# A decoder trunk in float32 on one core: the forget gates of its linear attention turned to features on partitions

## The chip, the core and the metric

One core of one Trainium2 chip runs the whole program in one launch. The metric is device time in microseconds, the median over several runs. Engines are named as the profile names them: PE is TensorE (matmuls; PEld its weight loads), ACT is ScalarE, DVE is VectorE, POOL is GpSimd, and SP issues the DMAs.

## The reference

Two layers over 16 meta tokens and 256 tokens of width 1024. Layer 0 is FFN, short convolution, FFN; layer 1 is FFN, gated linear attention (GLA), FFN; after each stands a residual with a layer norm. The change is in GLA alone, which has 4 heads with 128 key features each and chunks of 64 tokens:

```python
q, k, v, g, gz = jnp.split(h @ w_in, splits, axis=-1)
log_a = jax.nn.log_sigmoid((gz @ w_gate_up + b_gate).astype(f32)) / GLA_GATE_NORMALIZER   # / 16
...
b = jnp.cumsum(to_chunks(log_a, GLA_HEAD_K), axis=3)          # restarts in each chunk
b_ref = b[:, :, :, GLA_CHUNK // 2:GLA_CHUNK // 2 + 1, :]
b_last = b[:, :, :, -1:, :]
scores = jnp.einsum('nbhik,nbhjk->nbhij', q * jnp.exp(b - b_ref), k * jnp.exp(b_ref - b))
...
q_inter = q * jnp.exp(b)
k_state = k * jnp.exp(b_last - b)
decay = jnp.exp(b_last[:, :, :, 0, :])
# per chunk: o = q_inter @ state; state = decay * state + k_state^T v
```

The 272 tokens are one short chunk (the 16 meta tokens) and four chunks of 64.

## The kernel before

All activations lie transposed, features on partitions and tokens on the free axis. Every matrix product is done in three rounds with the operands split into a high and a low part (`hi`, `lo`), so a tile of 128 output features by 272 tokens takes 8 x 3 = 24 matmuls. The weights come as units of 128 x 1024: SP loads a unit into one of 4 raw buffers, ACT rounds it to `weights_hi` (L431, `split_hi`), DVE subtracts to get `weights_lo` (L753, `split_lo`), PE uses it (L1214 to L1216). Both split copies form a ring of 8 units, so unit j + 8 is split while the unit of tile j is used or gone. SP loads unit n as soon as `split_lo` of unit n - 4 is done. Every engine has its own instruction list in program order, with semaphores between them. Nothing reorders it: an instruction that waits holds all that stands behind it on its engine.

The GLA stage has 25 tiles, j = 0 to 24: j = 0 is the low-rank gate input gz, 1 to 4 the keys (`kT`), 5 to 8 the queries (`qT`, 256 tokens only), 9 to 16 the values, 17 to 24 the output gate. Tiles 0 to 3 are multiplied before the layer norm's statistics are known (L1239 to L1241, banks 0 to 3) and "unfolded" afterwards by DVE (L829 to L834); ACT then writes them out (L633), which counts in `gla_evac`, as the evacuation of each later tile does (L640, L642, L647). Tile 4 goes to PSUM bank 7, the tiles from 5 on to banks 0 and 1 in turn. So PE may begin tile j only when ACT has evacuated tile j - 2, by the wait for `gla_evac` ahead of each tile.

Between the tiles stand the steps of the gate. After tile 4 PE makes the gate logits with tokens on partitions (L1380: three matmuls of 512 columns, for 16, 128 and 128 tokens), DVE copies them out and takes -|x| (L1089, L1091), ACT does Exp (L662, at j = 5) and Ln(1 + x) (L666, at j = 6), DVE forms the log sigmoid (L1098, at j = 6), and PE sums it within chunks by a matmul with the triangular constant `cum` (L1391, at j = 9 to 11), which also turns the result to features on partitions. ACT copies the sums `b` out (L673); DVE forms the differences b - b_ref and b - b_last (L1109 to L1114, `differences`, at j = 9, 10, 11, 13); ACT takes five exponentials of them (L680 to L684, `decays`, at j = 9, 11, 13, 15), POOL multiplies q and k by them (L387 to L394), and PE goes on with turning v (L1399), turning k (L1410), the scores (L1417), the state updates (L1429) and the outputs.

Of the kernel before, what the change touches and what calls it, by code (L numbers as in the profile page):

```python
# [21 lines left out]
ALU = mybir.AluOpType  # L22
# [11 lines left out]
def hybrid_trunk(nc, x, meta_tokens, ln_gain, ln_bias, ffn_w_in, ffn_w_out, conv_w_in, conv_w,  # L34
# [37 lines left out]
    with ctx:  # L72
# [65 lines left out]
        log_a = gate_area[:, 0, 0:BLOCKS * DK].rearrange("p (b n) -> p b n", b=BLOCKS)  # L138
        soft = gate_area[:, 1, 0:BLOCKS * DK].rearrange("p (b n) -> p b n", b=BLOCKS)
        o_sb = gate_area[:, 0, 0:KD * SEQ].rearrange("p (m t) -> p m t", m=KD)  # L140
        silu_out = gate_area[:, 1, 0:KD * SEQ].rearrange("p (m t) -> p m t", m=KD)
        b_sb = h_f
# [18 lines left out]
        cum = sb("cum", [P, P])  # L161
# [35 lines left out]
        cum_made, b_copied, diffs_ready = sem("cum_made"), sem("b_copied"), sem("diffs_ready")  # L197
# [113 lines left out]
        def _(pool):  # L311
# [11 lines left out]
            for n in range(2):  # L323
                pool.wait_ge(hi_split, n + 1)
                if n:
# [5 lines left out]
            nc.gpsimd.memset(cum[:], 1.0 / 16.0).then_inc(ident_zeroed, 1)  # L331
            nc.gpsimd.memset(pick[:], 0.0).then_inc(pick_zeroed, 1)
            pool.wait_ge(ident_zeroed, 2)
            pool.wait_ge(masks_set, 1)
            nc.gpsimd.affine_select(out=cum[:], in_=cum[:], compare_op=ALU.is_ge, fill=0.0, base=0,
                                    pattern=[[1, P]], channel_multiplier=-1).then_inc(masks_set, 1)
            pool.wait_ge(masks_set, 2)
            nc.gpsimd.memset(cum[0:CH, CH:P], 0.0).then_inc(masks_set, 1)
            pool.wait_ge(pick_zeroed, 1)
            for h in range(HEADS):  # L340
                pool.wait_ge(masks_set, h + 3)
# [3 lines left out]
            pool.wait_ge(masks_set, 3 + HEADS)  # L345
# [79 lines left out]
        def _(act):  # L425
# [203 lines left out]
            def gla_tile(j):  # L629
# [8 lines left out]
                ps = bank[7 if j == FOLD else (j - 5) % 2]  # L638
# [9 lines left out]
                else:  # L648
                    m = j - 1 - 2 * HEADS - KD
                    if m == 0:  # L650
                        act.wait_ge(log_a_ready, 2)
# [4 lines left out]
            def softplus(stage):  # L656

                areas = [soft[0:META, 0, :], soft[:, 1:, :]]
                if stage == 0:
                    act.wait_ge(logits_folded, BLOCKS)  # L660
                    for a in areas:
                        nc.scalar.activation(a, a, ACT.Exp).then_inc(soft_step, 1)  # L662
                else:
                    act.wait_ge(soft_step, 2)
                    for a in areas:
                        nc.scalar.activation(a, a, ACT.Ln, bias=1.0).then_inc(soft_step, 1)  # L666

            def copy_b(h):
                act.wait_ge(cum_made, h + 1)
                if h >= 3:  # L670
                    act.wait_ge(exps_ready, 5 * (h - 2))
                    act.wait_ge(diffs_ready, 3 * (h - 2))
                nc.scalar.activation(b_sb[:, h % 3, :], bank[6 + h % 2][:, 0:T], ACT.Copy).then_inc(b_copied, 1)  # L673

            def decays(h):
# [4 lines left out]
                nc.scalar.activation(e_last[:], d_last[:, h % 2, :], ACT.Exp, scale=-1.0).then_inc(exps_ready, 1)  # L680
                nc.scalar.activation(e_buf[:, 0, :], d_ref[:, h % 3, :], ACT.Exp).then_inc(exps_ready, 1)
                nc.scalar.activation(e_buf[:, 1, :], d_ref[:, h % 3, :], ACT.Exp, scale=-1.0).then_inc(exps_ready, 1)
                nc.scalar.activation(e_buf[:, 2, :], b_sb[:, h % 3, META:T], ACT.Exp).then_inc(exps_ready, 1)
                nc.scalar.activation(decay[:, h, :], b_sb[:, h % 3, META - 1:KT0:CH], ACT.Exp).then_inc(exps_ready, 1)  # L684
# [31 lines left out]
            for j in range(GLA_TILES):  # L716
# [3 lines left out]
                if j == 5:  # L720
                    softplus(0)
                if j == 6:
# [3 lines left out]
                if j == 9:  # L726
                    copy_b(0)
                    copy_b(1)
                if j in (10, 11):
                    copy_b(j - 8)  # L730
# [17 lines left out]
        def _(dve):  # L748
# [335 lines left out]
            def copy_logits():  # L1084

                for b in range(BLOCKS):
                    r = slice(0, META if b == 0 else P)
                    dve.wait_ge(logits_made, b + 1)
                    nc.vector.tensor_copy(log_a[r, b, :], bank[4 + b][r, :]).then_inc(logits_copied, 1)  # L1089
                    dve.wait_ge(logits_copied, b + 1)  # L1090
                    nc.vector.scalar_tensor_tensor(out=soft[r, b, :], in0=log_a[r, b, :], scalar=-1.0, in1=log_a[r, b, :],  # L1091
                                                   op0=ALU.mult, op1=ALU.min).then_inc(logits_folded, 1)

            def log_sigmoid():

                dve.wait_ge(soft_step, 4)
                for a, s in [(log_a[0:META, 0, :], soft[0:META, 0, :]), (log_a[:, 1:, :], soft[:, 1:, :])]:
                    nc.vector.scalar_tensor_tensor(out=a, in0=a, scalar=0.0, in1=s, op0=ALU.min,  # L1098
                                                   op1=ALU.subtract).then_inc(log_a_ready, 1)

            def differences(h):

                s = h % 3
                dve.wait_ge(b_copied, h + 1)
                if h >= 2:
                    dve.wait_ge(exps_ready, 5 * (h - 1))
                b_main = b_sb[:, s, META:T].rearrange("p (c i) -> p c i", i=CH)
# [431 lines left out]
```

## Time and profile before

| | us |
|---|---|
| median of 3 runs (lowest to highest) | 1069.47 (1069.30 to 1069.88) |
| the profiled execution: device time | 1069.2 |
| its span, first to last instruction | 1067.5 |
| PE busy in it | 1042.2 (98%) |
| PEld, DVE, ACT, POOL busy | 1022.6, 727.9, 521.9, 130.4 |
| mean granted TensorE clock | 0.993 of full speed |
| raw tiles 0 to 3 and tile 4 of the GLA stage on PE | 716.4 to 733.1 |
| tiles 5 to 24 of the GLA stage on PE | 736.0 to about 835 |

A row of the timeline gives start, duration, engine, line and operation; in brackets stands how long the engine had been idle before and which instruction ended that. Busy times overlap on PE, because matmuls are pipelined: the pace of PE is read from start to start, not from the durations. The profiled execution's time stands 1.7 us above its span and 0.3 us below the median.

### The profile page before, as it was taken

The page shows a single profiled execution, that of the slowest core. Times are in us where ns is not written, and L with a number is a line of the kernel's source. Part 1 is how long each engine was busy: PE and PEld are TensorE (multiplying, and loading weights), DVE is VectorE, ACT ScalarE, POOL GpSimd, SP SyncE. Part 2 cuts the span into 40 slices and gives each one's busy share as a digit, 9 for nine tenths or more (in the row PEclk, how much of TensorE's full clock was granted, in tenths as well). Part 3 has the DMA queues.
Part 4 walks back from the last instruction along what each step waited for, and adds up shares of the span by engine and source line. Part 5 has one row for each costly group of instructions (what it writes and reads, how often), then busy time and mean ns, then how long its engine had stood idle before and what let it go on. Part 6 is the DMA issues. An engine that isn't in the chain of part 4 may idle for free.

```text
span 1067.5 us, 19769 instructions
## 1 busy us (share of the span) xinstructions
PE 1042.2 (98%) x8217; PEld 1022.6 (96%) x8217; DVE 727.9 (68%) x1097; ACT 521.9 (49%) x758; POOL 130.4 (12%) x149
## 2 busy tenths in 40 slices
PE   7999999999999999999999999998899999999996
PEld 5999999999999999999999999996888999999995
DVE  6765557689789755566895565767644899666644
ACT  4634444464456444344653343555745665444432
POOL 4000002220001000012300000322130220000132
PEclk9999999999999999999999999999999999999998
DMA  7866556628754866566386655562532528765631
GB/s 218 239 200 175 167 157 179 191 82 230 204 159 118 238 172 174 156 175 181 93 242 192 178 167 164 151 193 80 159 99 80 155 84 244 211 192 167 180 93 40
DMA packets 343722, 175.58 MB, mean 164 GB/s; under 512 B 6658, under 2 KB 342576, under 8 KB 343632
## 3 DMA queue, kind: packets, MB, share of 16 engines
q1 hardware_dynamic: 342992, 173.36, 56.7%
q8 instruction: 65, 1.06, 0.4%
q10 hardware_dynamic: 448, 0.85, 0.3%
q14 instruction: 25, 0.20, 0.1%
q0 software_dynamic: 192, 0.10, 0.0%
HBM read 173.24 MB, written 1.05 MB: 163 GB/s over the span
## 4 chain that ended last, share of the span: by engine, by line
PE 93%; DVE 3%; ACT 2%; DMA 1%; issue 1%; POOL 0%; SPq 0%; POOLq 0%; DVEq 0%; ACTq 0%
PE bank L1214 28%; PE bank L1216 28%; PE bank L1215 28%; PE bank L1239 2%; PE bank L1241 2%; PE bank L1240 2%; DVE weights_lo L753 1%; ACT weights_hi L431 1%; DMA raw_weights<-in_ffn_w_in_dram 1%; PE bank L1429 1%; PE bank L1446 1%; PE bank L1442 0%; PE bank L1455 0%; PE bank L1391 0%; DVE rstd L869 0%
## 5 line engine op out<-in xcount | busy, mean ns | idle before, releaser
L753 DVE TENSOR_TENSOR weights_lo<-raw_weights,weights_hi 128x1024 fp32r<-128x1024 f32 x335 | 415.8, 1246 | 236.5 <-ACT weights_hi L431 236.0
L431 ACT ACTIVATE weights_hi<-raw_weights 128x1024 fp32r<-128x1024 f32 x337 | 355.6, 1059 | 427.9 <-PE bank L1216 371.4
L1214 PE MATMUL bank<-x_hi,weights_hi 128*128 128x272 f32 (+1 forms) x1640 | 474.7, 289 | 8.2 <-ACT qT L642 8.2
L1216 PE MATMUL bank<-x_hi,weights_lo 128*128 128x272 f32 (+1 forms) x1640 | 472.0, 288 | 0.0
L1215 PE MATMUL bank<-x_lo,weights_hi 128*128 128x272 f32 (+1 forms) x1640 | 470.4, 287 | 0.0
L1214 PEld LDWEIGHTS bank<-x_hi,weights_hi 128*128 128x128 f32 x1640 | 310.0, 189 | 12.9 <-ACT qT L642 8.8
L1215 PEld LDWEIGHTS bank<-x_lo,weights_hi 128*128 128x128 f32 x1640 | 310.1, 189 | 0.0
L1216 PEld LDWEIGHTS bank<-x_hi,weights_lo 128*128 128x128 f32 x1640 | 309.9, 189 | 0.0
L1216 PE MATMUL bank<-mid_hi,weights_lo 128*128 128x272 f32 (+1 forms) x704 | 202.0, 287 | 0.0
L1214 PE MATMUL bank<-mid_hi,weights_hi 128*128 128x272 f32 (+1 forms) x704 | 201.6, 286 | 0.0
L1215 PE MATMUL bank<-mid_lo,weights_hi 128*128 128x272 f32 (+1 forms) x704 | 201.1, 286 | 0.0
L1214 PEld LDWEIGHTS bank<-mid_hi,weights_hi 128*128 128x128 f32 x704 | 132.7, 189 | 0.0
L1215 PEld LDWEIGHTS bank<-mid_lo,weights_hi 128*128 128x128 f32 x704 | 132.6, 188 | 0.0
L1216 PEld LDWEIGHTS bank<-mid_hi,weights_lo 128*128 128x128 f32 x704 | 132.3, 188 | 0.0
L356 POOL TENSOR_TENSOR total<-resid 128x272 f32<-128x272 f32 (+1 forms) x4 | 3.5, 880 | 570.4 <-DVE resid L781 570.4
L946 DVE TENSOR_TENSOR prod<-bank,silu_g 128x272 f32<-128x272 f32 (+1 forms) x82 | 35.8, 436 | 48.8 <-PE bank L1216 48.8
L374 POOL TENSOR_TENSOR resid<-resid,mean 128x272 f32<-128x272 f32 (+1 forms) x47 | 38.5, 855 | 150.6 <-ACT mean L468 150.6
L1239 PE MATMUL bank<-zg_hi,weights_hi 128*128 128x274 f32 (+1 forms) x160 | 47.2, 295 | 0.0
L1241 PE MATMUL bank<-zg_hi,weights_lo 128*128 128x274 f32 (+1 forms) x160 | 46.2, 289 | 0.0
L1240 PE MATMUL bank<-zg_lo,weights_hi 128*128 128x274 f32 (+1 forms) x160 | 46.0, 288 | 0.0
L952 DVE TENSOR_TENSOR mid_lo<-prod,mid_hi 128x272 fp32r<-128x272 f32 (+1 forms) x88 | 38.6, 439 | 3.0
L361 POOL TENSOR_TENSOR total_sq<-total_sq,sq 128x272 f32<-128x272 f32 (+1 forms) x24 | 38.9, 1620 | 0.5
(189 smaller groups left out, 911.5 us busy)
## 6 DMA issues: line engine op xcount, KB each, us to landing
raw_weights<-in_ffn_w_in_dram SPq DMA_DIRECT2D x176, 512.0 KB, 4.0
raw_weights<-in_ffn_w_out_dram SPq DMA_DIRECT2D x64, 512.0 KB, 3.8
raw_weights<-in_ffn_w_out_dram SPq DMA_DIRECT2D x32, 384.0 KB, 3.4
raw_weights<-in_conv_w_in_dram SPq DMA_DIRECT2D x24, 512.0 KB, 3.8
raw_weights<-in_gla_w_in_dram SPq DMA_DIRECT2D x24, 512.0 KB, 3.8
raw_weights<-in_conv_w_out_dram SPq DMA_DIRECT2D x8, 512.0 KB, 4.8
raw_weights<-in_gla_w_out_dram SPq DMA_DIRECT2D x8, 512.0 KB, 3.8
out_dram<-out_tok SPq DMA_DIRECT2D x3, 256.0 KB, 2.1
```

Of the source, the lines that this page charges most:

```text
L361: nc.gpsimd.tensor_tensor(total_sq[:, cols], total_sq[:, cols], sq[:, mo % 2, cols], ALU.add).then_inc(totals_ready, 1)
L374: nc.gpsimd.tensor_tensor(resid[:, k, cols], resid[:, k, cols], mean[:, cols], ALU.subtract).then_inc(centred, 1)
L431: nc.scalar.activation(w_hi[:, n % RING, :], raw[:, n % RAW, :], ACT.Copy).then_inc(hi_split, 1)
L753: nc.vector.tensor_tensor(w_lo[:, s, :], raw[:, n % RAW, :], w_hi[:, s, :].bitcast(F32), ALU.subtract).then_inc(lo_split, 1)
L946: nc.vector.tensor_tensor(prod[:, s, cols], bank[2 * (t % PAIRS) + 1][:, 0:n_tok], silu_g[:, s, cols], ALU.mult).then_inc(prod_ready, 1)
L952: nc.vector.tensor_tensor(mid_lo[:, at_t, cols], prod[:, s:s + 1, cols], mid_hi[:, at_t, cols].bitcast(F32), ALU.subtract).then_inc(mid_re ...
L1214: nc.tensor.matmul(ps, w_h, hi[:, k, cols], start=first and k == k0, stop=False)
L1215: nc.tensor.matmul(ps, w_h, lo[:, k, cols], start=False, stop=False)
L1216: mm = nc.tensor.matmul(ps, w_l, hi[:, k, cols], start=False, stop=last and k == k1 - 1)
L1239: nc.tensor.matmul(ps, w_h, zg_hi[:, k, cols], start=k == 0, stop=False)
L1240: nc.tensor.matmul(ps, w_h, zg_lo[:, k, cols], start=False, stop=False)
L1241: mm = nc.tensor.matmul(ps, w_l, zg_hi[:, k, cols], start=False, stop=k == KD - 1)
```

## The change

Parts of the diff, shortened. Line numbers of the new kernel are lower by 4 on ACT and by 14 on DVE up to this stage. The gate logits are made with features on partitions, one matmul of 272 columns per head. The running sums are made by DVE with one scan per head over the 272 tokens; `restart` is 1, and 0 at each chunk's first token, and is multiplied with the running value. The division by 16 goes into the scale of the exponentials. The matmuls with `cum` and ACT's copies of the sums are gone. DVE does the three unfoldings in a row. The tiles up to 9 use banks 0, 1 and 2 in turn, so PE waits up to tile 11 for one evacuation fewer, and Exp and Ln move one tile later on ACT.

```diff
+        def tile_bank(j):
+            return (j - 4) % 3 if j < 10 else j % 2
...
# tensor engine
-                for b in range(BLOCKS):
-                    r = slice(0, META) if b == 0 else slice(META + (b - 1) * P, META + b * P)
-                    nc.tensor.matmul(bank[4 + b][0:r.stop - r.start, :], gzT[:, r], gate_up[:], start=True,
+                for h in range(HEADS):
+                    nc.tensor.matmul(bank[4 + h][:, 0:T], gate_up[:, h * P:(h + 1) * P], gzT[:], start=True,
                                      stop=True).then_inc(logits_made, 1)
-            def cumulate(h):
-                pe.wait_ge(log_a_ready, 2)
...
-                    mm = nc.tensor.matmul(bank[6 + h % 2][:, r], log_a[0:size, b, h * P:(h + 1) * P],
-                                          cum[0:size, 0:size], start=True, stop=True)
...
             def turn_v(v):
                 pe.wait_ge(gla_evac, 2 + 2 * HEADS + v)
+                if v == 0:
+                    pe.wait_ge(logits_copied, HEADS)
...
-                if j > FOLD:
-                    pe.wait_ge(gla_evac, j - 4 if j < 7 else j - 1)
+                pe.wait_ge(gla_evac, j - 3 if j < 7 else j - 2 if j < 12 else j - 1)
# scalar engine
-            def copy_b(h):
...
             def copy_o(h):
                 act.wait_ge(o_made, h + 1)
+                act.wait_ge(scanned, HEADS)
...
-                if j == 5:
+                if j == 6:
                     softplus(0)
-                if j == 6:
+                if j == 7:
                     softplus(1)
...
-                if j == 9:
-                    copy_b(0)
-                    copy_b(1)
# vector engine
+            def fold_logits():
+                for h in range(HEADS):
...
+                    nc.vector.tensor_copy(log_a[:, h, :], ps).then_inc(logits_copied, 1)
...
+                    nc.vector.scalar_tensor_tensor(out=soft[:, h, :], in0=log_a[:, h, :], scalar=-1.0, in1=log_a[:, h, :],
+                                                   op0=ALU.mult, op1=ALU.min).then_inc(logits_folded, 1)
+            def run_sums(h):
...
+                dve.wait_ge(log_a_ready, h + 1)
+                nc.vector.tensor_tensor_scan(out=b_sb[:, h, :], data0=restart[:], data1=log_a[:, h, :], initial=0.0,
+                                             op0=ALU.mult, op1=ALU.add).then_inc(scanned, 1)
...
-                if 0 < j < FOLD:
-                    unfold(FFN_NORM[2], n0, j, T)
+                if j == 0:
+                    for u in range(1, FOLD):
+                        unfold(FFN_NORM[2], n0, u, T)
                 if j < GLA_TILES - 1:
                     split_lo(n0 + j + RING)
                 if j == 4:
-                    copy_logits()
+                    fold_logits()
                 if j == 6:
-                    log_sigmoid()
+                    nc.vector.memset(restart[:], 1.0).then_inc(restart_set, 1)
+                    dve.wait_ge(restart_set, 1)
+                    nc.vector.memset(restart[:, 0:1], 0.0).then_inc(restart_set, 1)
+                    nc.vector.memset(restart[:, META:T:CH], 0.0).then_inc(restart_set, 1)
+                if j in (7, 8):
+                    for h in (2 * j - 14, 2 * j - 13):
+                        log_sigmoid(h)
+                        run_sums(h)
```

DVE, from the end of the layer norm to the logits, before. The rows `weights_lo` are `split_lo`, here of units 7 and 8 and then of units 9 and 10; three rows make one unfolding (of tile 1 from bank 1, of tile 2 from bank 2):

```order
L753 TENSOR_TENSOR weights_lo<-raw_weights,weights_hi 128x1024 x2
L829 SCALAR_TENSOR_TENSOR unfolded<-mean,bank1 128x272
L832 COPY fold_bias<-bank1 128x1
L834 TENSOR_TENSOR unfolded<-unfolded,rstd 128x272
L753 TENSOR_TENSOR weights_lo<-raw_weights,weights_hi 128x1024
L829 SCALAR_TENSOR_TENSOR unfolded<-mean,bank2 128x272
L832 COPY fold_bias<-bank2 128x1
L834 TENSOR_TENSOR unfolded<-unfolded,rstd 128x272
L753 TENSOR_TENSOR weights_lo<-raw_weights,weights_hi 128x1024
```

The same place now:

```order
L739 TENSOR_TENSOR weights_lo<-raw_weights,weights_hi 128x1024
L815 SCALAR_TENSOR_TENSOR unfolded<-mean,bank1 128x272
L818 COPY fold_bias<-bank1 128x1
L820 TENSOR_TENSOR unfolded<-unfolded,rstd 128x272
L815 SCALAR_TENSOR_TENSOR unfolded<-mean,bank2 128x272
L818 COPY fold_bias<-bank2 128x1
L820 TENSOR_TENSOR unfolded<-unfolded,rstd 128x272
L815 SCALAR_TENSOR_TENSOR unfolded<-mean,bank3 128x272
L818 COPY fold_bias<-bank3 128x1
L820 TENSOR_TENSOR unfolded<-unfolded,rstd 128x272
L739 TENSOR_TENSOR weights_lo<-raw_weights,weights_hi 128x1024 x5
```

The unfoldings of tiles 1, 2 and 3 stand together ahead of the split of unit 8; the splits of units 8 to 12 follow in a row.

DVE from the splits of units 13 and 14 (the first row) to the first differences, before; L1098 is the log sigmoid, then come the splits of units 15 to 17:

```order
L753 TENSOR_TENSOR weights_lo<-raw_weights,weights_hi 128x1024 x2
L1098 SCALAR_TENSOR_TENSOR gate_area<-gate_area 16x512
L1098 SCALAR_TENSOR_TENSOR gate_area<-gate_area 128x1024
L753 TENSOR_TENSOR weights_lo<-raw_weights,weights_hi 128x1024 x3
L1109 TENSOR_TENSOR scaled<-h_f 128x256
L1111 TENSOR_TENSOR d_last<-h_f 128x192
L1114 TENSOR_TENSOR d_last<-h_f 128x16
```

Now, from the first log sigmoid on (L1083, with L1091 the scan; `shift` is the tensor that serves as `restart`), with the splits of units 16 and 17 between them:

```order
L1091 SCALAR_TENSOR_TENSOR gate_area<-shift,gate_area 128x272
L1083 SCALAR_TENSOR_TENSOR gate_area<-gate_area 128x272
L1091 SCALAR_TENSOR_TENSOR gate_area<-shift,gate_area 128x272
L739 TENSOR_TENSOR weights_lo<-raw_weights,weights_hi 128x1024
L1083 SCALAR_TENSOR_TENSOR gate_area<-gate_area 128x272
L1091 SCALAR_TENSOR_TENSOR gate_area<-shift,gate_area 128x272
L1083 SCALAR_TENSOR_TENSOR gate_area<-gate_area 128x272
L1091 SCALAR_TENSOR_TENSOR gate_area<-shift,gate_area 128x272
L739 TENSOR_TENSOR weights_lo<-raw_weights,weights_hi 128x1024
L1102 TENSOR_TENSOR scaled<-gate_area 128x256
L1104 TENSOR_TENSOR d_last<-gate_area 128x192
L1107 TENSOR_TENSOR d_last<-gate_area 128x16
```

Eight instructions of 272 elements have taken the place of two; the scans stand in DVE's list between the splits.

ACT from the evacuation of tile 5 on, before (L642 evacuates a query tile, L662 is Exp, L666 the table load and Ln):

```order
L642 ACTIVATE qT<-bank0 128x256
L431 ACTIVATE weights_hi<-raw_weights 128x1024
L662 ACTIVATE gate_area<-gate_area 16x512
L662 ACTIVATE gate_area<-gate_area 128x1024
L642 ACTIVATE qT<-bank1 128x256
L431 ACTIVATE weights_hi<-raw_weights 128x1024
L666 ACT_TABLE_LOAD
L666 ACTIVATE gate_area<-gate_area 16x512
L666 ACTIVATE gate_area<-gate_area 128x1024
```

Now (L638 evacuates, L658 is Exp, L661 the table load and Ln):

```order
L638 ACTIVATE qT<-bank1 128x256
L427 ACTIVATE weights_hi<-raw_weights 128x1024
L638 ACTIVATE qT<-bank2 128x256
L427 ACTIVATE weights_hi<-raw_weights 128x1024
L658 ACTIVATE gate_area<-gate_area 128x544 x2
L638 ACTIVATE qT<-bank0 128x256
L427 ACTIVATE weights_hi<-raw_weights 128x1024
L661 ACT_TABLE_LOAD
L661 ACTIVATE gate_area<-gate_area 128x544 x2
```

Tile 6 is evacuated ahead of Exp and tile 7 ahead of Ln, where before tile 6 stood behind Exp and tile 7 behind Ln.

## Rows read from the trace of the kernel before

**Rows 1.** PE's waits over the whole span: total us, times, longest us

```profile
PE bank L1214 <- ACT qT L642: 8.2, 3, 6.3
...
PE bank L1508 <- ACT resid L476: 4.7, 4, 4.2
```

**Rows 2.** timeline of PE, tiles 5 to 8 (start us, us, engine, line, operation)

```profile
733.14 2.94 PE L1380 MATMUL bank<-gate_up,gzT 17*16 17x512 f32 x6
736.01 0.39 PE L1214 MATMUL bank<-x_hi,weights_hi 128*128 128x256 f32 x1
...
748.18 0.58 PE L1214 MATMUL bank<-x_hi,weights_hi 128*128 128x256 f32 x1 [6.26 <-ACT qT L642]
...
752.33 0.28 PE L1216 MATMUL bank<-x_hi,weights_lo 128*128 128x256 f32 x1
753.49 0.39 PE L1214 MATMUL bank<-x_hi,weights_hi 128*128 128x256 f32 x1 [0.88 <-ACT qT L642]
...
756.28 0.28 PE L1216 MATMUL bank<-x_hi,weights_lo 128*128 128x256 f32 x1
```

**Rows 3.** windows (engines' busy us, then granted clock, DMA share, GB/s)

```profile
744.00:745.00 1.00, 0.00 (x0) 0.00 (x0) 0.00 (x0) 1.00 (x2) 0.00 (x0) 0.67 0.81 216
750.00:751.00 1.00, 1.00 (x7) 1.00 (x6) 0.96 (x3) 0.00 (x0) 0.00 (x0) 0.50 1.10 312
1058.00:1059.00 1.00, 0.37 (x2) 0.29 (x2) 1.00 (x3) 0.58 (x2) 1.00 (x2) 0.68 0.00 0
```

**Rows 4.** timeline of ACT, tiles 4 to 11

```profile
746.36 1.28 ACT L719 ACT_TABLE_LOAD   x1
...
747.76 0.37 ACT L642 ACTIVATE qT<-bank 128x256 f32<-128x256 f32 x1
...
764.43 0.38 ACT L680 ACTIVATE e_last<-d_last 128x208 f32<-128x208 f32 x1 [1.19 <-DVE d_last L1114]
...
765.63 0.19 ACT L684 ACTIVATE decay<-h_f 128x4 f32<-128x4 f32 x1
...
766.16 1.05 ACT L431 ACTIVATE weights_hi<-raw_weights 128x1024 fp32r<-128x1024 f32 x1
...
767.54 0.36 ACT L693 ACTIVATE v_tok<-bank 128x256 f32<-128x256 f32 x1
```

**Rows 5.** timeline of PE, two plain float32 matmuls of 272 columns

```profile
718.47 0.62 PE L1221 MATMUL bank<-total,meanD 128*128 128x272 f32 x2
718.93 0.62 PE L1226 MATMUL bank<-total_sq,meanD 128*128 128x272 f32 x2
```

**Rows 6.** timeline of PE, tile 10 and tile 12

```profile
760.81 1.99 PE L1391 MATMUL bank<-cum,gate_area 16*128 16x16 f32 x12
762.56 0.37 PE L1214 MATMUL bank<-x_hi,weights_hi 128*128 128x272 f32 x1
...
771.97 0.37 PE L1214 MATMUL bank<-x_hi,weights_hi 128*128 128x272 f32 x1
```

**Rows 7.** timeline of DVE, before tile 5

```profile
732.43 1.22 DVE L753 TENSOR_TENSOR weights_lo<-raw_weights,weights_hi 128x1024 fp32r<-128x1024 f32 x1
734.20 1.23 DVE L753 TENSOR_TENSOR weights_lo<-raw_weights,weights_hi 128x1024 fp32r<-128x1024 f32 x1 [0.55 <-ACT weights_hi L431]
735.34 0.50 DVE L829 SCALAR_TENSOR_TENSOR unfolded<-mean,bank 128x272 f32<-128x272 f32 x1
...
735.87 0.44 DVE L834 TENSOR_TENSOR unfolded<-unfolded,rstd 128x272 f32<-128x272 f32 x1
```

**Rows 8.** weight loads of this stage, issue to landing

```profile
DMA to landing us min/median/max: 3.7/3.9/5.3
```

**Rows 9.** instructions of DVE by shape, 720 to 768 us (busy us, mean ns)

```profile
L869 DVE RECIPROCAL rstd<-std 128x272 f32<-128x272 f32 x1 | 1.9, 1852 | 0.6 <-ACT std L470 0.6
...
L1091 DVE SCALAR_TENSOR_TENSOR gate_area<-gate_area 128x512 f32<-128x512 f32 x2 | 1.4, 694 | 0.1
...
L863 DVE TENSOR_TENSOR var<-bank,mean_sq 128x272 f32<-128x272 f32 x1 | 0.4, 442 | 0.8 <-PE bank L1226 0.8
```

More of the change, by code:

```diff
@@ L160, in hybrid_trunk @@
         gate_up = sb("gate_up", [RANK + 1, DK])
-        cum = sb("cum", [P, P])
         pick = sb("pick", [P, P])
@@ L637, in gla_tile @@
                 act.wait_ge(unit_used, n0 + j + 1)
-                ps = bank[7 if j == FOLD else (j - 5) % 2]
+                ps = bank[tile_bank(j)]
                 if j <= HEADS:
@@ L656, in softplus @@
             def softplus(stage):
[L658 to L661, printed above, removed]
+                for pair in range(2):
+                    a = soft[:, 2 * pair:2 * pair + 2, :]
+                    if stage == 0:
+                        act.wait_ge(logits_folded, 2 * pair + 2)
                         nc.scalar.activation(a, a, ACT.Exp).then_inc(soft_step, 1)
-                else:
-                    act.wait_ge(soft_step, 2)
-                    for a in areas:
+                    else:
+                        act.wait_ge(soft_step, pair + 1)
                         nc.scalar.activation(a, a, ACT.Ln, bias=1.0).then_inc(soft_step, 1)
-            def copy_b(h):
[L669 to L673, printed above, removed]
             def decays(h):
@@ L679, in decays @@
                     act.wait_ge(decayed, 2 * h)
[L680 to L684, printed above, removed]
+                rate = 1.0 / 16.0
+                nc.scalar.activation(e_last[:], d_last[:, h % 2, :], ACT.Exp, scale=-rate).then_inc(exps_ready, 1)
+                nc.scalar.activation(e_buf[:, 0, :], d_ref[:, h % 3, :], ACT.Exp, scale=rate).then_inc(exps_ready, 1)
+                nc.scalar.activation(e_buf[:, 1, :], d_ref[:, h % 3, :], ACT.Exp, scale=-rate).then_inc(exps_ready, 1)
+                nc.scalar.activation(e_buf[:, 2, :], b_sb[:, h, META:T], ACT.Exp, scale=rate).then_inc(exps_ready, 1)
+                nc.scalar.activation(decay[:, h, :], b_sb[:, h, META - 1:KT0:CH], ACT.Exp,
+                                     scale=rate).then_inc(exps_ready, 1)
             def copy_v(v):
@@ L1094, in log_sigmoid @@
[L1094 to L1099, printed above, removed]
+            def fold_logits():
+                for h in range(HEADS):
+                    dve.wait_ge(logits_made, h + 1)
+                    ps = bank[4 + h][:, 0:T]
+                    nc.vector.tensor_copy(log_a[:, h, :], ps).then_inc(logits_copied, 1)
+                    dve.wait_ge(logits_copied, h + 1)
+                    nc.vector.scalar_tensor_tensor(out=soft[:, h, :], in0=log_a[:, h, :], scalar=-1.0, in1=log_a[:, h, :],
+                                                   op0=ALU.mult, op1=ALU.min).then_inc(logits_folded, 1)
@@ L1425, in outers @@
                     pe.wait_ge(state_ready, NC * h)
-                else:
-                    pe.wait_ge(b_copied, HEADS)
                 for c in range(NC):
```

61 lines of the change are left out of this document (20 added, 41 removed).

## The prediction

> **What bounds the kernel now.** I read the shares of busy time first: PE is busy 98% of the span, so only PE work that disappears and PE waits that disappear count. The list of PE's waits comes next: over the whole span its largest entry is PE held by ACT's evacuations of query tiles, 8.2 us in three waits, the longest 6.3 (the second row here, 4.2 us, is the end of the program) [rows 1]. PE's timeline places them [rows 2]: tile 7 begins at 748.18 after 6.26 us of silence, tile 8 after 0.88, tile 9 after 1.03. The silence costs a second time. The granted clock fell to half (1.2 of 2.4 GHz) inside it and was still there at 750 to 751 us [rows 3], so tile 7 took 4.15 us from its first to its last matmul where tile 8 took 2.79 [rows 2]: 1.36 us. Behind the first wait stands a slow circle: unfolding on DVE, `kT` and `split_hi` on ACT, `split_lo` on DVE, and only then the next unfolding, so ACT reaches tile 5 at 747.76 [rows 4] though PE had finished it at about 739.
>
> **The change part by part.**
>
> *PE work removed.* The three logit matmuls of 512 columns run from 733.14 to 736.01, 2.87 us [rows 2]. Now there are four of 272 columns; two such float32 matmuls start 0.46 us apart [rows 5], so 4 x 0.46 = 1.84, and with the gap of 0.1 before the next tile PE is at tile 5 at 735.1: 0.9 us gained. The sums by matmul take 760.81 to 762.56 for two heads, 1.75 us [rows 6]; for four, 3.5 us are gone.
>
> *PE waits.* I lay out the new timetable from the unchanged instant 733.14, with paces of before: a query tile 2.79 us to its last matmul and 0.13 more, 2.92 [rows 2]; a tile of 272 columns 3.15, longer by its columns and the gap at the end. Tiles 5, 6 and 7 run without a wait to 743.9, if ACT has evacuated tile 4 by 741.0, and tile 8 if it has evacuated tile 5 by 743.9.
>
> ACT and DVE: `split_lo` of unit 7 starts at 732.43 and holds DVE for 1.14 us (734.20 to 735.34 is the same step) [rows 7], to 733.57. Three unfoldings follow; one takes 0.53 to its last instruction and then 0.40 [rows 7], 0.93, so 2.8 for three: 736.3. `split_lo` of unit 8 then ends at 737.5, where it ended at 735.4 before. This moved step counts, since SP's load of unit 12 waits for it and lands 3.9 us later [rows 8], at 741.4; ACT's `split_hi` of unit 12 stands there and holds all behind it. ACT has evacuated tile 4 before that, near 739, so tile 7 is free. After the split (1 us) and the table load of 1.28 us plus 0.1 [rows 4], ACT evacuates tile 5 at 743.8 to 744.15: tile 8 waits 0.3 us. Tiles 8 and 9 then run to 750.2 and tile 10 to 753.4.
>
> Now DVE is the queue that counts. It cannot fold the logits before `split_lo` of unit 12, 742.5 to 743.65. Then, without a pause:
> - four copies and folds of 272: 0.45 + 0.41 (a read of a bank with 272 elements takes 442 ns [rows 9]; the fused form takes 0.50, of which about 0.09 lie under the next instruction [rows 7]), 3.4 us, to 747.1;
> - units 13 and 14, 2.3; three memsets, 0.45 by the count of elements; unit 15, 1.1: to 751.0. ACT has Exp done by 747.8, loads the table and has the first Ln by 750.9, so it holds nobody up;
> - four log sigmoids of 0.53 (0.50 [rows 7], then the scan's start behind it) and four scans, with unit 16 behind the second: to 757.1 with the scan at 0.78;
> - unit 17, 1.1, and the first differences, 0.8: 759.0.
>
> The scan is in no row. Nothing excludes that it costs as much as the fused form (two operations in one pass) of the same size, 0.50 us [rows 7]; from above I bound it by the slowest row of this size, the reciprocal, 1.85 us [rows 9]. I take 0.78: nearer to the fused form, because the operations and operands are alike, but above it, because each element must wait for the sum before it. Its cost counts four times.
>
> The Trainium skill has a rule for just this ("DVE: opcode table, instruction layouts, handler registers and perf-mode slots", section Datapath and trigger behaviour): the built-in scan routes its result back to an earlier stage and runs at half throughput. No row shows a scan. The fused form at 512 and 272 elements, 694 and about 500 ns [rows 7, 9], shows 0.81 ns per element; doubled, a scan would be 0.50 + 272 x 0.81 ns = 0.72 us, and the total 0.2 us lower than with my value.
>
> PE reaches turn_v(0) at 753.4. It needs the evacuation of tile 9, which stands on ACT behind Ln, tile 8 and another table load, and ends at 754.35: a wait of 1.0. Tile 11 then ends at 757.9. turn_v(1) needs the copy of v behind `decays(0)` on ACT, and `decays(0)` is the wait that matters: ACT stands before it from 755.2 to 759.0, with the evacuation of tile 10, a split and the copy of v queued behind. The five exponentials take 1.3 us (764.43 to 765.63 and the last one), the evacuation 0.3, the split 1.0, the two copies 0.5 [rows 4]: 762.1. So PE is silent from 757.9 to 762.1, **4.2 us, a new wait in the place of the old one**. By then POOL has multiplied k and nearly q and k by their decays (it starts at 759.4 and needs 3 us), so turn_k and the scores follow at once; tile 12 starts 1.06 us later, at 763.2.
>
> Before, tile 12 started at 771.97 [rows 6]. The same reckoning with the old program gives 771.75, so I add 0.2: 763.4, a gain of 8.6 us. As a sum of terms: 0.9 + 3.5 of work, 8.2 of waits and 1.36 of clock go, 14.0; 0.3 + 1.0 + 4.2 = 5.5 come: 8.5. From tile 12 on the order is unchanged on all engines but for ACT's copies of sums, which are gone. DVE and ACT wait for PE there, so the rest moves up whole. POOL's triangular constant at the start, the new waits on `scanned` and `exps_ready` and the pass through the other bank cost or give nothing: what they wait for is over by microseconds. The memsets alone stand in DVE's queue, and there they are counted.
>
> *The clock.* The old silence of 6.3 us began with the end of tile 6 at 741.9 and lost the clock at about 744.3 (the window from 744 has 0.67, a third of a microsecond at full speed [rows 3]), after 2.4 us. At the end of the program PE is silent for 4.2 us up to 1058.6 [rows 1], and the clock falls at about 1058.4 by the same reading [rows 3], after 4 us. A silence of 4.2 us stands between the two. I take it as falling, at the price that tile 7 paid: 1.36 us given back on tile 12. The sum is 8.6 - 1.4 = 7.2 us. 1069.2 for the profiled execution becomes 1062.0; its median stands 0.3 higher: **1062.3 us**.
>
> **The rivals.**
> - *The clock stays, or the scan is as fast as the fused form.* The short distance to the row at the end of the program speaks for the first. Without the fall 1060.9; with a scan of 0.50 the new silence shrinks by 4 x 0.28 = 1.1 to 3.1 us, which makes a stay likelier: 1059.8.
> - *The scan costs as much as the reciprocal.* DVE is the queue that counts, so 4 x 1.07 = 4.3 us more of silence: 1066.6. The serial dependence speaks for it; against it, the reciprocal is another kind of operation.
> - *The wait only moves: nothing measurable is gained.* The chain logits, Exp, Ln, sums, differences, decays might be as late as before for a cause that I don't see, say loads that crowd each other when DVE frees four raw buffers within 4 us (a landing took up to 5.3 us [rows 8]). It would have to eat 5 us, and the landing that counts, of unit 12, is the first of the four. About 1068.5.
> - *Slower.* One mechanism: the scan at a price per element above everything seen. PE's silence at turn_v(1) grows by four times the excess; the 7.2 us are used up when a scan takes 0.78 + 7.2/4 = 2.6 us, 9.5 ns an element, where the reciprocal has 6.8. At 3.5 us a scan the time is 1062.3 + 10.9 = 1073.2. No row comes near.
>
> **How the numbers follow.** The forecast has 0.5 (its own range 1061 to 1064), the clock or fast scan 0.27, the scan as the reciprocal 0.1, the moved wait 0.08, slower 0.05. The range goes from the fast scan with the clock kept, 1059.3, to the slow scan, 1067.0; outside lie most of the last two and little else. A change of 0.2% is about what a measurement of this kernel can tell from none, 2.1 us, so 1067.3 is the border of faster: the first three cases are below it, with a part of the fourth, 0.89; no change 0.06, slower 0.05.
>
> **What would show it right or wrong.** No L1391 of `cum` and no wait before tile 7; PE's largest wait of the stage ahead of turn_v(1), on ACT's copy of v, near 4 us; ACT idle ahead of the first of the five exponentials for 3 to 4 us, ended by DVE's differences; DVE without a pause from the split of unit 12 to there; ACT waiting some 2 us for the landing of unit 12; tile 12 at 763 to 765; a window at half clock around 762 or none. The prediction is wrong if PE finds a wait of more than a microsecond elsewhere, if ACT and not DVE is late before the first exponentials, or if the scan is far from 0.8 us.

## The result and the profile after

| | before | changed |
|---|---|---|
| median (lowest to highest), us | 1069.43 (1069.30 to 1069.88), 4 runs | 1063.21 (1062.26 to 1063.65), 4 runs |
| profiled execution: device time, span | 1069.2, 1067.5 | 1062.88, 1061.1 |
| PE busy | 1042.2 | 1039.6 |
| DVE busy | 727.9 | 729.2 |

The ratio given with the result is 0.9936, 95% interval 0.9924 to 0.9948 (the quotient of the two medians is 0.9942): faster by 6.2 us by the medians, 0.6%. 1062.3 was forecast.

The list of PE's waits of the changed kernel, same view as [rows 1], whole span:

```profile
...
PE bank L1490 <- ACT resid L472: 4.7, 4, 4.2
PE bank L1389 <- ACT v_tok L683: 3.6, 1, 3.6
...
PE bank L1407 <- POOL qT L390: 0.5, 1, 0.5
PE bank L1389 <- ACT prod L643: 0.4, 1, 0.4
```

The 8.2 us ahead of query tiles are gone, and one wait of 3.6 us ahead of turn_v(1) (L1389) has come. A second of 0.5 us, ahead of the scores (L1407) for POOL's product (L390), was in no term of the forecast. PE's timeline, where [rows 2] stood for before:

```profile
733.64 2.10 PE L1380 MATMUL bank<-gzT,gate_up 17*128 17x272 f32 x8
735.67 0.39 PE L1215 MATMUL bank<-x_hi,weights_hi 128*128 128x256 f32 x1
...
755.27 0.28 PE L1389 MATMUL bank<-ident,prod 128*16 128x128 f32 x1 [0.42 <-ACT prod L643]
...
762.39 0.27 PE L1389 MATMUL bank<-ident,prod 128*16 128x128 f32 x1 [3.60 <-ACT v_tok L683]
...
762.72 0.49 PE L1400 MATMUL bank<-ident,k_st 128*16 128x128 f32 x3
763.72 1.22 PE L1407 MATMUL bank<-q_pos,kT 128*128 128x128 f32 x4 [0.52 <-POOL qT L390]
...
764.60 0.57 PE L1215 MATMUL bank<-x_hi,weights_hi 128*128 128x272 f32 x1
...
769.16 1.75 PE L1417 MATMUL bank<-v_tok,k_tok 16*128 16x256 f32 x8
```

The last steps of this stretch (turn_k, scores, first state update) in the kernel before:

```profile
771.27 0.49 PE L1410 MATMUL bank<-ident,k_st 128*16 128x128 f32 x3
771.60 0.61 PE L1417 MATMUL bank<-q_pos,kT 128*128 128x128 f32 x4
...
775.48 0.69 PE L1429 MATMUL bank<-v_tok,k_tok 16*128 16x256 f32 x2
```

Logits start to tile 5 is 2.03 us where it was 2.87. Tile 12 stands at 764.60, against 771.97 in [rows 6]: 7.4 us earlier. Its first matmul has 0.57 us against 0.37: the clock is low. Windows of the changed kernel (columns as in [rows 3]; the third number from the right is the granted clock, behind POOL's):

```profile
736.00:737.00 1.00, 1.00 (x8) 1.00 (x7) 1.00 (x4) 1.00 (x3) 0.00 (x0) 0.59 1.11 333
738.00:739.00 1.00, 1.00 (x6) 1.00 (x6) 1.00 (x1) 1.00 (x2) 0.00 (x0) 0.50 0.00 0
...
763.00:764.00 1.00, 0.48 (x3) 0.28 (x2) 1.00 (x3) 0.89 (x3) 0.67 (x1) 0.75 0.00 0
765.00:766.00 1.00, 1.00 (x6) 1.00 (x6) 1.00 (x4) 0.73 (x4) 0.00 (x0) 0.50 1.14 346
```

The fall near 763.5 is the forecast one, 4.7 us after the end of tile 11 (758.8) and 1.1 us after the silence was over; from 767 us on the granted clock is 1.00 again. The one from 736 to 740, in tile 5, is not: it comes while PE is fully busy. DVE's timeline from the split of unit 12 to the first differences (`shift` is the tensor that serves as `restart`):

```profile
743.23 1.23 DVE L739 TENSOR_TENSOR weights_lo<-raw_weights,weights_hi 128x1024 fp32r<-128x1024 f32 x1 [1.88 <-ACT weights_hi L427]
744.38 0.43 DVE L1075 COPY gate_area<-bank 128x272 f32<-128x272 f32 x1
744.84 0.44 DVE L1077 SCALAR_TENSOR_TENSOR gate_area<-gate_area 128x272 f32<-128x272 f32 x1
...
753.33 0.72 DVE L1091 TENSOR_TENSOR_SCAN gate_area<-shift,gate_area 128x272 f32<-128x272 f32 x1
753.97 1.20 DVE L739 TENSOR_TENSOR weights_lo<-raw_weights,weights_hi 128x1024 fp32r<-128x1024 f32 x1
...
759.01 0.17 DVE L1107 TENSOR_TENSOR d_last<-gate_area 128x16 f32<-128x16 f32 x1
761.86 1.23 DVE L739 TENSOR_TENSOR weights_lo<-raw_weights,weights_hi 128x1024 fp32r<-128x1024 f32 x1 [2.68 <-ACT weights_hi L427]
763.00 0.95 DVE L1102 TENSOR_TENSOR scaled<-gate_area 128x256 f32<-128x256 f32 x1
```

No row behind 743.23 has a bracket up to 759.01, so DVE never waits there: this queue sets the end of the differences. A scan takes 0.72 us (0.64 from its start to the next instruction's). ACT's timeline shows both of its waits at the ends of that queue, for the landing of unit 12 and for the differences:

```profile
742.14 1.06 ACT L427 ACTIVATE weights_hi<-raw_weights 128x1024 fp32r<-128x1024 f32 x1 [2.60 <-DMA raw_weights<-in_gla_w_in_dram]
...
759.21 0.38 ACT L669 ACTIVATE e_last<-d_last 128x208 f32<-128x208 f32 x1 [3.04 <-DVE d_last L1107]
...
761.89 0.36 ACT L683 ACTIVATE v_tok<-bank 128x256 f32<-128x256 f32 x1
```

And POOL's:

```profile
761.26 0.73 POOL L388 TENSOR_TENSOR kT<-kT,silu_g 128x256 f32<-128x256 f32 x1
761.95 1.72 POOL L390 TENSOR_TENSOR qT<-qT,silu_g 128x256 f32<-128x256 f32 x1
...
769.74 0.72 POOL L390 TENSOR_TENSOR qT<-qT,silu_g 128x256 f32<-128x256 f32 x1
```

A product of 256 elements takes 0.73 us at 761.26 and 1.72 at 761.95, the latter beside DVE's split at 761.86; the same line takes 0.72 again at 769.74, while DVE has a pause (up to 770.31). The differences at 763.00 take 0.95 where the same ones took 0.42 at 758.41, on an idle POOL. The split itself keeps its usual 1.23. The rows add up as if each waited for the other's whole instruction: the split holds DVE until 763.00, POOL's product ends 0.67 us later, at 763.67, and the differences 0.28 later, at 763.95. No run was made to test this reading.

### The profile page after: what moved, and what is told of

It is laid out like the page before. It is cut to its first block, busy times and chain, and to the rows that moved or that the text cites. A ratio compares the mean times of both kernels' runs of the same rounds, so it can differ in the third digit from the quotient of the medians.

```text
span 1061.1 us, 19729 instructions
## 1 busy us (share of the span) xinstructions
PE 1039.6 (98%) x8195; PEld 1022.4 (96%) x8195; DVE 729.2 (69%) x1108; ACT 519.8 (49%) x754; POOL 130.1 (12%) x146
## 4 chain that ended last, share of the span: by engine, by line
PE 93%; DVE 3%; ACT 2%; DMA 1%; POOL 1%; issue 0%; SPq 0%; POOLq 0%; DVEq 0%; ACTq 0%
PE bank L1215 28%; PE bank L1217 28%; PE bank L1216 28%; PE bank L1240 2%; PE bank L1242 2%; PE bank L1241 2%; DMA raw_weights<-in_ffn_w_in_dram 1%; DVE weights_lo L739 1%; ACT weights_hi L427 1%; PE bank L1417 1%; PE bank L1434 1%; PE bank L1430 0%; PE bank L1443 0%; DMA raw_weights<-in_gla_w_in_dram 0%; DVE rstd L855 0%
```

## The experiments

All are medians with their lowest and highest, each compared with the kernel before on the same chip: 1069.67 for e1 to e4, 1069.76 for e5 to e8, 1069.88 for e9 to e11. Differences from the changed kernel are taken from its 1063.21; measured again as e11, on another chip, it has 1063.47. Theory: DVE's queue from unit 12 to the first differences sets one wait of PE, which took the place of the old circle of unfoldings and splits, and the scan counts four times in it.

**The unfoldings, one by one again** (e1, in the changed kernel):

```diff
-                if j == 0:
-                    for u in range(1, FOLD):
-                        unfold(FFN_NORM[2], n0, u, T)
+                if 0 < j < FOLD:
+                    unfold(FFN_NORM[2], n0, j, T)
```

> The changed kernel, with the three unfoldings one by one between the splits as before; all else as changed. Theory (VectorE's queue from the split of unit 12 to the first differences sets PE's wait at turn_v(1), and that queue starts when unit 12 has landed): the circle of unfolding, kT, split_hi, split_lo holds unit 12 and the fold of the logits back by some 4 us; tile 12 starts 3.8 us later, PE waits ahead of tiles 5 to 7 and still near 3.6 us at turn_v(1): 1067 us. Rival (the three banks and the scans bring the gain, the order of the unfoldings is covered by PE's later wait): no more than 1 us lost, 1064.

1066.54 us (1065.35 to 1067.67), ratio 0.9971 [0.9960, 0.9982]. PE's waits in the stage:

```profile
PE bank L1388 <- ACT v_tok L683: 3.6, 1, 3.6
PE bank L1214 <- ACT kT L629: 1.7, 1, 1.7
PE bank L1214 <- ACT kT L636: 1.1, 1, 1.1
```

The wait ahead of turn_v(1) is unchanged and the old circle is back as 2.8 us ahead of tiles 5 and 7. (The wait ahead of turn_v(0) is 1.0 us, 0.6 more than in the changed kernel.) The three unfoldings in a row are worth 3.3 us.

**Each scan twice** (e2):

```diff
+                nc.vector.tensor_tensor_scan(out=b_sb[:, h, :], data0=restart[:], data1=log_a[:, h, :], initial=0.0,
+                                             op0=ALU.mult, op1=ALU.add).then_inc(scan_twice, 1)
+                dve.wait_ge(scan_twice, h + 1)
```

> The changed kernel with each of the four scans done twice (same values). Theory: all four stand in the queue that PE waits for, each costs 0.7 us, so PE's silence at turn_v(1) grows from 3.6 to 6.4 us and the time to 1066.0. Rival (ACT's table loads and Ln pace the chain, VectorE only follows): less than 1 us, since only scans behind the last Ln count; 1064.

1065.67 us (1065.26 to 1066.63), ratio 0.9963 [0.9949, 0.9978]: 2.5 us slower than the changed kernel.

```profile
PE bank L1393 <- ACT v_tok L684: 6.6, 1, 6.6
```

The wait grew from 3.6 by 3.0 us. DVE's stretch from the split of unit 12 to the last difference grew by as much, from 15.95 to 18.98 us: a second scan starts 0.76 us behind the first, four times. DVE's queue sets the wait, and there the scan has its full price. In the time 2.5 of the 3.0 are left, since POOL's product no longer holds the scores (0.5 us).

**The schedule without the gate** (e3): the kernel before, with only the unfoldings in a row and the third bank with its shorter waits.

```diff
-                if j > FOLD:
-                    pe.wait_ge(gla_evac, j - 4 if j < 7 else j - 1)
+                pe.wait_ge(gla_evac, j - 3 if j < 7 else j - 2 if j < 12 else j - 1)
```

> The kernel before with only the unfoldings in a row and the tiles over three banks with the shorter waits; gate logits and sums as before. Theory: unit 12 lands earlier in the same way, the silence of 6.3 us and its clock loss go; waits of about 1.9 us before tile 9 and 2.4 us before the sums come; tile 12 starts 5.6 us earlier than before: 1063.8 us, so nearly the whole gain. Rival (the gain is the PE work of the sums and the logits and the chain by scans): 1067 or more.

1066.38 us (1066.30 to 1068.01), ratio 0.9972 [0.9961, 0.9984]: 2.6 above the theory's number and 0.6 below the rival's. The main wait is one of 2.40 us ahead of the sums. The timeline of PE and the windows show what the reckoning lacked:

```profile
756.45 2.72 PE L1395 MATMUL bank<-cum,gate_area 16*128 16x16 f32 x12 [2.40 <-DVE gate_area L1101]
```

```profile
757.00:758.00 1.00, 1.00 (x7) 0.84 (x6) 1.00 (x2) 1.00 (x1) 0.00 (x0) 0.69 0.00 0
758.00:759.00 1.00, 1.00 (x6) 1.00 (x6) 0.66 (x1) 0.99 (x4) 0.00 (x0) 0.50 0.11 18
```

The silence ended at 756.45, yet the clock fell at 757.4, after the small matmuls of the sums had begun, and stayed low to 760.8; those matmuls took 2.72 us where they took 1.99 [rows 6]. From their start to the next matmuls of `cum`, one tile later, it is 6.44 us, where it was 4.95 in the kernel before: the clock lost about 1.5 us here, and a second fall at 737 stands in tile 5. The logits began 0.9 us later than in the kernel before (734.05), with no wait ahead of them.

**The first differences earlier** (e4): right after the first scan (j = 7), ahead of the other three heads.

```diff
                         run_sums(h)
-                if j in (9, 10, 11, 13):
+                        if h == 0:
+                            differences(0)
+                if j in (10, 11, 13):
```

> The changed kernel with the first head's differences moved on VectorE from behind the split of unit 17 to right behind the first scan. Theory: ACT finds them ready when it comes to the first exponentials (755.2 in place of 759.2), PE's wait at turn_v(1) shrinks from 3.6 to about 0.5 us, the clock stays at 2.4 GHz: 3.2 + 1.3 us less, 1058.7 us. Rival (ACT's own queue or POOL's products are as late): the wait moves to turn_k or the scores and less than 1 us is gained, 1062.5.

**1058.89 us** (1058.76 to 1059.17), ratio 0.9899 [0.9885, 0.9914]: 4.3 us below the changed kernel. Taking the differences out from behind DVE's queue took PE's wait for v from 3.6 to 0.4 us. What is left is POOL's:

```profile
PE bank L1409 <- POOL qT L390: 1.2, 1, 1.2
...
PE bank L1391 <- ACT v_tok L683: 0.4, 1, 0.4
```

```profile
756.48 1.02 POOL L383 TENSOR_TENSOR k_st<-kT,e_last 128x208 f32<-128x208 f32 x1 [29.49 <-ACT e_last L669]
757.46 0.94 POOL L386 TENSOR_TENSOR q_pos<-qT,silu_g 128x256 f32<-128x256 f32 x1
758.36 1.14 POOL L388 TENSOR_TENSOR kT<-kT,silu_g 128x256 f32<-128x256 f32 x1
759.47 1.70 POOL L390 TENSOR_TENSOR qT<-qT,silu_g 128x256 f32<-128x256 f32 x1
```

```profile
756.35 0.72 DVE L1091 TENSOR_TENSOR_SCAN gate_area<-shift,gate_area 128x272 f32<-128x272 f32 x1
756.99 0.81 DVE L1083 SCALAR_TENSOR_TENSOR gate_area<-gate_area 128x272 f32<-128x272 f32 x1
757.84 1.15 DVE L1091 TENSOR_TENSOR_SCAN gate_area<-shift,gate_area 128x272 f32<-128x272 f32 x1
758.91 3.34 DVE L739 TENSOR_TENSOR weights_lo<-raw_weights,weights_hi 128x1024 fp32r<-128x1024 f32 x2
```

Once POOL works, a log sigmoid goes from 0.42 to 0.81 us, a scan from 0.72 to 1.15, two splits from 2.35 (at 747.69 in the changed kernel, beside an idle POOL) to 3.34; POOL's products are slower likewise. That both engines lose fits the reading above, in which they take turns.

**Two banks' waits** (e5): each tile from 7 on waits again for the evacuation two tiles back.

```diff
-                pe.wait_ge(gla_evac, j - 3 if j < 7 else j - 2 if j < 12 else j - 1)
+                pe.wait_ge(gla_evac, j - 3 if j < 7 else j - 1)
```

> The changed kernel, with PE waiting ahead of tiles 7 to 11 for the evacuation of tile j - 2 as before, so that the third bank buys nothing. Theory: PE stands some 3 us ahead of tile 7 (table load and tile 5's evacuation on ACT) but only 1.5 us at turn_v(1), because that silence ends by VectorE's and ACT's queue and not by when PE arrives; tile 12 starts at the same time: 1063 us, at most 1 us less if no silence is long enough to lose the clock on the path. Rival (the third bank is part of the gain): 1066.

1063.58 us (1062.36 to 1064.58), ratio 0.9942 [0.9929, 0.9956]: the same as the changed kernel. PE's waits are now 3.5 us ahead of tile 7 and 1.8 ahead of turn_v(1), where the changed kernel has 3.6 in one. But the silence is not only moved. The trace is of the slowest of the four executions (1064.58), and in it DVE's queue has two pauses that the changed kernel's has not:

```profile
751.33 1.23 DVE L739 TENSOR_TENSOR weights_lo<-raw_weights,weights_hi 128x1024 fp32r<-128x1024 f32 x1 [0.44 <-ACT weights_hi L427]
...
753.30 0.44 DVE L1083 SCALAR_TENSOR_TENSOR gate_area<-gate_area 128x272 f32<-128x272 f32 x1 [0.74 <-ACT gate_area L661]
```

ACT was late there because it had stood 0.94 us for tile 7, which PE ran late and, from 745.1 to 748.5, at half clock:

```profile
749.96 0.39 ACT L638 ACTIVATE qT<-bank 128x256 f32<-128x256 f32 x1 [0.94 <-PE bank L1217]
```

turn_v(1) began at 764.00 instead of 762.39. So DVE's queue sets when turn_v(1) can go, and a PE that is late enough at tile 7 pushes that queue back by 1.2 us in this execution. The medians do not show this cost; whether the third bank is worth nothing or up to 1 us stays open.

**The silence filled** (e6) with 16 matmuls of 512 columns, whose result nobody reads:

```diff
+                if v == 1:
+                    pe.wait_ge(lo_split, n0 + 13)
+                    keep_warm(n0 + 12, 16)
```

> The changed kernel with 16 matmuls of 512 columns on real weights put ahead of turn_v(1), into a bank that nobody reads (3.4 us of the 3.6 us silence; same output). Theory: the clock stays at 2.4 GHz through tile 12, which takes 3.0 us in place of 4.0, and the scores gain 0.3: 1.3 us less, 1061.9. Rival (the clock loss is covered by something later, or the extra matmuls delay turn_v): 1063.2 or more.

1061.30 us (1061.20 to 1061.78), ratio 0.9923 [0.9910, 0.9935]: 1.9 us below the changed kernel. The granted clock is 1.00 in the windows around the filling (758 to 759, 760 to 761) and from 762 to 766, and the first state update stands at 767.85 instead of 769.16: 1.3 us earlier. The other 0.6 us is of the size of the differences between runs of one kernel.

**The logits in two halves** (e7), on top of the first differences earlier: heads 0 and 1 behind tile 4, heads 2 and 3 behind tile 5.

```diff
-                if j == 4:
-                    logits()
+                if j in (4, 5):
+                    logits((0, 1) if j == 4 else (2, 3))
```

> The kernel with the first differences early (1058.9), and of the four logit matmuls two behind tile 4 and two behind tile 5. Theory (the block of four matmuls on 17 rows, 2 us, with the gaps beside it is what lets the clock fall at tile 5 in most executions, and with PE's long wait gone that loss is on the path): tile 5 runs at 2.4 GHz: 1057.6. Rival (the fall at tile 5 has another cause or is covered): 1058.9.

1059.24 us (1058.80 to 1059.72), ratio 0.9902 [0.9889, 0.9916]: nothing gained. The clock fell at 736.4 all the same. A new wait of 0.8 us for tile 1's evacuation stood ahead of tile 5, so the run does not tell whether the sparse logits or the wait did it; e8, which has the same split logits and the same wait (0.8 us), has no fall there.

**The scores wait only for POOL's product of the keys** (e8), on top of that (`decayed` is counted after POOL's last product, which the scores don't read; `kq_ready` is a new semaphore, counted after the product of the keys):

```diff
-                pe.wait_ge(decayed, 2 * h + 2)
+                pe.wait_ge(kq_ready, h + 1)
```

> As the kernel with early differences and spread logits, and the scores wait for POOL's product of k (a semaphore of its own) and no longer for that of q with exp(b), which comes behind it and takes 1.7 us beside VectorE. Theory (PE's last wait of the stage, 1.2 us ahead of the scores, is for that product): 1.2 us less, 1056.4. Rival (the wait moves to the next step): 1057.6.

1060.08 us (1058.44 to 1061.39), ratio 0.9912 [0.9897, 0.9928]: above both numbers. The four executions lie apart, 1058.44 and 1059.03 against 1061.12 and 1061.39; the trace is of 1059.03, and what cost the other two 2 us is not known. In the trace the mechanism is the rival's. The scores went at 759.75, 1.5 us earlier than in e4, and PE met the wait at the next step, the state updates, for DVE's copy of the turned keys:

```profile
PE bank L1420 <- DVE k_tok L1116: 1.6, 1, 1.6
```

**And that copy first in DVE's list** (e9, the logits in one piece again): the copies of keys and scores of head 0 ahead of the split at j = 11.

```diff
+                if j == 11:
+                    copy_k(0)
+                    copy_scores(0)
...
-                if j in (11, 13, 15, 17):
+                if j in (13, 15, 17):
```

> e4_diff_early with two more edits: the scores of a head wait only for POOL's product of the keys (new semaphore), and on DVE the copies of the turned keys and of the scores for head 0 stand ahead of the split of unit j + 8 at j = 11, not behind it and the differences of head 1. Theory: what is left of e4's wait is DVE's queue at j = 11; e8, with the short scores wait alone, moved PE's wait to the outer products (1.6 us for DVE's copy of the keys). With both, the outer products go at once: PE's waits ahead of scores and outers together under 0.5 us (1.2 in e4), outers 0.8 to 1.5 us earlier than e4's 765.4, time 1057.4 to 1058.2. Rival: the split of unit 19, now later, delays the loads or a later tile, and gives it back: 1058.9 or above, with a new wait of PE for ACT or DVE after 766.

**1058.40 us** (1058.06 to 1058.54), ratio 0.9893 [0.9876, 0.9909]: between the two numbers by the median, the theory's by the trace.

```profile
759.46 0.27 PE L1395 MATMUL bank<-ident,prod 128*16 128x128 f32 x1 [0.45 <-ACT v_tok L684]
...
760.11 0.61 PE L1413 MATMUL bank<-q_pos,kT 128*128 128x128 f32 x4
...
764.00 1.75 PE L1423 MATMUL bank<-v_tok,k_tok 16*128 16x256 f32 x8
```

Neither scores nor state updates wait; the latter stand at 764.00, 1.4 us ahead of e4's, and the span is 1056.3 against 1057.4. By the medians the step from e4 is 0.5 us, by the ratios, whose intervals overlap, 0.6: the time alone does not show it. Both e4 and e9 are faster than the changed kernel.

**The gate without the schedule** (e10): the changed kernel with the unfoldings one by one and the two banks' waits, so e1's and e5's edits together.

> The changed kernel's gate (logits with features on partitions, scans, no sums by matmul) without the rest of the schedule: unfoldings one by one between the splits as before, and each tile from 7 on waits for the evacuation of the tile two back. Theory (work removed counts whole, waits stay as in e1): logits 0.9 and sums 3.5 go, a wait at tile 5 or 7 of 2 to 3 us stays ahead of the table load, and turn_v(1) waits 3 to 4 us: 1066 to 1067, as e1. Rival: the gate part is the whole gain and the schedule adds nothing: 1063.2. Second rival: without the schedule the gate part gains nothing because the 4.4 us of matmuls become waits: 1069.5.

1066.29 us (1066.11 to 1067.66), ratio 0.9970 [0.9959, 0.9981]: the time as the theory had it, the waits not. They are larger ahead of tiles 5 and 7 and smaller ahead of turn_v(1) than was expected (the trace is of the slowest execution, 1067.66; the clock was at half from 737.6 to 741.0 and from 747.8 to 754.6):

```profile
PE bank L1214 <- ACT qT L638: 3.9, 1, 3.9
PE bank L1388 <- ACT v_tok L683: 1.7, 1, 1.7
PE bank L1214 <- ACT kT L629: 1.7, 1, 1.7
```

The gate part alone is worth 3.6 us, the schedule alone 3.3 (e3), both together 6.2 to 6.4: two shares that nearly add up, with nothing from the third bank that the medians show: e10, which lacks it, gained 3.6 where e1 gained 3.1, and e5 6.2 like the changed kernel. The later place of Exp and Ln on ACT is in e10 and not in e3; no run has it alone.

**The changed kernel again** (e11), on the chip of e9 and e10:

> The changed kernel as it is, on the same chip as the others of this batch: 1063.2 (1062.3 to 1064), ratio 0.994. If it lies outside, the small differences of the other runs (e5, e7, e8) can't be read at half a microsecond.

1063.47 us (1062.65 to 1064.33), ratio 0.9940 [0.9925, 0.9955]. The median is in the expected band, the highest execution 0.3 us above it.

## Why the prediction was right

The time was 0.9 us above the forecast, inside its own range, and the mechanism was the forecast one: the old waits gone, one new wait that DVE's queue sets. Step by step:

- *The removed work.* Logits: 0.84 us gained between their start and tile 5, forecast 0.9. Sums: no matmul of `cum` is left; in the kernel before they took 3.5 us.
- *The old waits.* Gone, with their clock loss. e1 shows that the unfoldings in a row did it.
- *The new wait ahead of turn_v(1).* In place and for the reason given: DVE without a pause from 743.23, differences done at 759.2 (forecast 759.0), v copied at about 762.3 (762.1). It is 3.6 us, not 4.2, because PE came later than reckoned (tile 11 ended at 758.8, forecast 757.9), through logits that began 0.5 us later and the unforeseen half clock in tile 5. The loss in tile 5 cost nothing: it shortened a wait that DVE's queue ends. e4 took the wait away by taking one step out of that queue.
- *The small waits.* Ahead of turn_v(0) 0.4 us, forecast 1.0, and none ahead of tile 8, forecast 0.3; both are swallowed by PE's late arrival.
- *The scan.* 0.72 us, taken at 0.78. The estimate that the Trainium skill ("DVE: opcode table, instruction layouts, handler registers and perf-mode slots", Datapath and trigger behaviour: half throughput for the scan) gave from the fused form's pace was 0.72; this trace agrees with it. The pace under it had mixed a pass that reads a bank (0.50) with one from SBUF (694 ns); with the 0.44 us of a pass from SBUF the same estimate gives 0.73, so the agreement does not hang on that. One size was measured, so the price per element is not shown. e2 shows that its cost counts in full, four times, in PE's wait.
- *The clock.* The fall came. From the scores to the first state update the changed kernel takes 5.44 us (763.72 to 769.16), with the silence filled 3.99 (763.86 to 767.85): a price of 1.45 us, forecast 1.36, 0.4 of it already in the scores. The rival in which the clock stays, 1060.9, is what e6's 1061.3 looks like.
- *The mis-sized terms.* The first state update stands 6.3 us earlier than before (769.16 against 775.48) and the end 6.4; 7.2 was forecast. The 0.9 is made of three pieces. The largest is POOL's last product, slowed by DVE: from turn_k to the scores it is 1.00 us (762.72 to 763.72) where it was 0.33 before (771.27 to 771.60), 0.7 more, 0.5 of it marked as PE's wait. The sum had put POOL beside an idle DVE, at 0.73 us a product, and so had no term for this. The Trainium skill ("GPSIMD Engine Reference", Specifications) names the contention: POOL shares its SBUF interfaces with DVE, against DVE's instructions with two SBUF inputs. The traces agree, with POOL's 1.72 us beside a split and e4's rows for the DVE side. The second piece: turn_v(1) began at 762.39 instead of 762.1, 0.3 us, most of which the 0.2 us covers that the forecast had added to its timetable. The third: the clock's price is 0.1 larger. Behind the 0.3 stand two things that nearly cancel: DVE's queue began 0.7 us late (743.23 against 742.5) and took 0.5 less, since a scan holds it for 0.64 us and not 0.78; that near agreement is luck. Most of the lateness is no work of the change: the logits began at 733.64 instead of 733.14, and the matmul that is the hundredth from the first tile's start stands 0.5 us later already (29.51 against 29.03). At the start of the program PE's matmuls of 272 columns start 0.23 us apart where later it is 0.13, up to 17.1 us in the trace of before and 19.2 in this one; over the traces of e1 to e8 this end lies between 16.8 and 19.9, and the logits begin between 733.3 and 734.5. How the one goes with the other is not shown. The forecast took one execution's 733.14 as fixed; it is the earliest of all the traces here.
- *The rivals.* The scan as slow as the reciprocal is ruled out by 0.72 us, the slower case with it. The wait that only moves was seen elsewhere: in e8 it went to the next step, in e5 it was split in two. The bottom of the range, 1059.3, was said to be the fast scan with the clock kept, which the same text reckons at 1059.8; nothing hangs on the difference.

What stays open: why the clock falls in tile 5, on a busy PE, in some executions (it begins between 735.6 and 737 and lasts 3.3 to 3.5 us, in the changed kernel, e3, e4, e6, e7, e11) and not in others (the kernel before, e2, e5, e8, e9). In e1 and e10 it falls there too, at the end of a wait of 1.7 us ahead of the tile. PE's instructions up to that place do not decide it: the changed kernel, e6 and e11 have the same ones as e2 and e5, and e7 the same as e8. In the changed kernel the fall is hidden; e8 and e9, whose traces lack it, don't show what it would cost there.

## What to carry to other kernels

When a wait goes, follow the queue that is late next to its last step and look for the one instruction in it that the waiting engine needs: moving that step to the front (e4, 4.3 us) was worth more than the gate's new form alone (3.6). Ask of a wait that is left whether its semaphore counts more than the reader needs, and whether the step behind it is ready too, or the wait will only move on by one (e8 against e9). A price taken from an engine's row holds for the neighbours it had in that row: DVE and POOL side by side on float32 paid up to double and more.

## What the runs showed of the hardware

- The multiply-add scan over 128x272 float32 takes 0.72 us, against 0.42 to 0.44 for a two-operation pass of the same size from SBUF.
- DVE and POOL slow each other: POOL 0.73 to 1.72 us for one product, DVE 0.42 to 0.95 for differences of 256 elements and 0.72 to 1.15 for a scan. The times fit two engines that take turns by whole instructions.
- In e3 the clock fell to 0.50 about 1 us after a silence of only 2.4 us had ended, with small matmuls running, and in e5 1.6 us after one of 1.8 us; in the kernel before it fell inside a silence of 6.3 us, 2.4 us after its start. The short gap of e3, followed by sparse work, cost 1.5 us, as much as the long one (1.36).
